# Chunk stage of an RWKV-7 time mix: inverse levels on the 32 changed columns, masks applied while leaving PSUM

## What is computed

```
def step(S, inp):
    r_t, w_t, k_t, v_t, a_t, b_t = inp
    sa = jnp.einsum('bhij,bhj->bhi', S, a_t)
    S = (S * w_t[:, :, None, :] + sa[..., None] * b_t[:, :, None, :]
         + v_t[..., None] * k_t[:, :, None, :])
    return S, jnp.einsum('bhij,bhj->bhi', S, r_t)

seq_in = tuple(u.transpose(1, 0, 2, 3) for u in (r_h, w_h, k_h, v_h, -kk, kk * a_h))
S0 = jnp.zeros((B, N_HEADS, HEAD_DIM, HEAD_DIM), jnp.float32)
_, y = lax.scan(step, S0, seq_in)
```

## Time and profile before

| | us |
|---|---|
| median of three runs | 1816.76 (1816.45 to 1817.86) |
| the profiled execution | 1815.43 |
| its span in the trace | 1813.7 |
| TensorE busy | 1668.9 (92%) |
| VectorE busy | 868.4 (48%) |
| ScalarE busy | 609.5 (34%) |
| GpSimd busy | 227.0 (13%) |

### The profile page before, as it was taken

The page is one execution under the profiler, slowest core; times in us unless marked ns, Lnnn a source line. Parts: engine busy times, 40 slices in busy tenths (PEclk is TensorE's granted clock), DMA queues, the critical chain, the costliest instruction groups (busy, mean ns, idle before and its releaser), DMA issues. The chain is left out here.

```text
span 1813.7 us, 35585 instructions
## 1 busy us (share of the span) xinstructions
PE 1668.9 (92%) x15964; PEld 1513.4 (83%) x15964; DVE 868.4 (48%) x1089; ACT 609.5 (34%) x826; POOL 227.0 (13%) x238
## 2 busy tenths in 40 slices
PE   4999998999999999989999688788877999999997
PEld 3999897899999999879989687778735888888886
DVE  3454453344433443467565466545575544334432
ACT  2454353332221223255664222212143333222222
POOL 2010010001000104000002232322111011001100
PEclk9999997899999999979899899989988999999998
DMA  3211110233332323242221100000012333323331
GB/s 96 67 57 53 59 53 18 71 94 91 90 99 82 91 86 108 61 143 70 68 72 47 49 3 3 3 3 3 3 45 69 94 93 102 96 81 95 102 104 48
DMA packets 214169, 121.38 MB, mean 67 GB/s; under 512 B 8744, under 2 KB 209600, under 8 KB 213760
## 3 DMA queue, kind: packets, MB, share of 16 engines
q1 hardware_dynamic: 213712, 118.98, 22.3%
q10 hardware_dynamic: 304, 0.08, 0.0%
HBM read 112.29 MB, written 6.76 MB: 66 GB/s over the span
## 5 line engine op out<-in xcount | busy, mean ns | idle before, releaser
L124 ACT ACTIVATE w_hi<-w_raw 128x1024 fp32r<-128x1024 f32 (+1 forms) x194 | 215.5, 1111 | 603.8 <-PE psg L731 483.0
L731 PE MATMUL psg<-x_hi,w_hi 128*128 128x264 f32 (+1 forms) x1096 | 357.7, 326 | 9.3 <-PEq L2398 9.3
L731 PE MATMUL psg<-x_lo,w_hi 128*128 128x264 f32 (+1 forms) x1096 | 357.9, 327 | 0.0
L731 PE MATMUL psg<-x_hi,w_lo 128*128 128x264 f32 (+1 forms) x1096 | 356.9, 326 | 0.0
L128 DVE TENSOR_TENSOR w_lo<-w_raw,w_hi 128x1024 fp32r<-128x1024 f32 (+1 forms) x194 | 250.4, 1291 | 139.0 <-ACT w_hi L124 138.8
L731 PEld LDWEIGHTS psg<-x_hi,w_hi 128*128 128x128 f32 x1096 | 206.5, 188 | 29.0 <-issue 10.3
L731 PEld LDWEIGHTS psg<-x_lo,w_hi 128*128 128x128 f32 x1096 | 206.5, 188 | 18.3 <-issue 0.2
L731 PEld LDWEIGHTS psg<-x_hi,w_lo 128*128 128x128 f32 x1096 | 207.1, 189 | 17.6
L731 PE MATMUL psg<-mid_hi,w_hi 128*128 128x264 f32 (+1 forms) x451 | 146.3, 324 | 0.0
L731 PE MATMUL psg<-mid_lo,w_hi 128*128 128x264 f32 (+1 forms) x451 | 146.0, 324 | 0.0
L731 PE MATMUL psg<-mid_hi,w_lo 128*128 128x264 f32 (+1 forms) x451 | 145.7, 323 | 0.0
(11 more groups left out here) (362 smaller groups left out, 3431.0 us busy)
## 6 DMA issues: line engine op xcount, KB each, us to landing
w_raw<-in_w_ffn_in_dram SPq DMA_DIRECT2D x88, 512.0 KB, 3.8
w_raw<-in_w_ffn_out_dram SPq DMA_DIRECT2D x32, 704.0 KB, 4.5
w_raw<-in_w_qkv_dram SPq DMA_DIRECT2D x24, 512.0 KB, 3.7
w_raw<-in_w_rkv_dram SPq DMA_DIRECT2D x24, 512.0 KB, 3.9
w_raw<-in_w_o_attn_dram SPq DMA_DIRECT2D x8, 512.0 KB, 4.1
w_raw<-in_w_o_rwkv_dram SPq DMA_DIRECT2D x8, 512.0 KB, 3.9
v_first<-v_pair SPq DMA_DIRECT2D x8, 264.0 KB, 2.1
res_kept<-res SPq DMA_DIRECT2D x1, 2112.0 KB, 7.8
```

Of the source, the lines that this page charges most:

```text
L124: k.nc.scalar.activation(k.w_hi[j][:, 0:kt, :], k.raw[j][:, 0:kt, :], ACT.Copy).then_inc(k.hi_ready[j].h, 1)
L731: done = k.nc.tensor.matmul(k.psg[:, 2 * j + c, 0:size], w[:, t, :], x, start=t == first and n == 0, stop=t == last and n == 2)
```

## The change

In the chunk stage:

- The products of a level are made only for the 32 columns (of 64) that the level changes: xt changes in the right block of each pair of blocks, xs in the left one. `block_cols` picks them as the moving operand, so that 64 stationary columns meet 32 moving ones. At level 3 the xs product has 16 moving columns and 64 stationary ones, where it was 32x32.
- The mask is no longer put on L before the product, by GpSimd, but on T after it: VectorE's `next_t` multiplies T with the mask `cross` on its way out of PSUM into `turned`, whose other half stays zero. The tiles `turned` and half of `vc` are cleared once, by GpSimd. ScalarE's copies of T are gone except at level 4 (`quarter`). `low` itself is the stationary operand.
- `l_products` makes three products a head instead of two: the odd columns of L transposed, the even columns of L (32 each, for the first xt and xs) and all of L. The identity's columns in xt and xs are written by ScalarE (`eyes`), at the end of the step before.
- `turn_v` becomes eight full transposes. ScalarE takes over the copies of V and of y.
- Other PSUM banks. The opening products wait for y and the first state update of the step before, no longer for the last xt and av.
- Another order: `chain_w` after level 0's first half, `chain_u` after level 1's first half, `chain_y_state` after level 1, `chain_s` ahead of level 4. On VectorE `products` comes behind the state's updates, and `quads` is split into `keys` and `reads`.
- `across` returns its rows unchanged: the products of a head stay in the rows of that head.

The diff, cut to its core:

```diff
@@ def chunk_stage(k, r):
+        def across(rows):
+
+            return rows
...
@@ ScalarE, step
-                        copy_t(n, 0)
+                        act.wait_ge(tv_d.h, n + 1)
+                        nc.scalar.activation(uv[p][C:P, :, :].rearrange("p (two m) c -> p m two c", two=2),
+                                             pair_ps[C:P].rearrange("p b (m two c) -> p (b m) two c", two=2, c=C), ACT.Copy)\
+                            .then_inc(uvv_r.h, 1)
...
@@ GpSimd, step
-                    if prep:
-                        pool.wait_ge(low_r.h, n + 1)
-                        for e in range(levels_of(n)):
-                            nc.gpsimd.tensor_tensor(es[e][:], low[:], over_rows(ch.level[e + 1]),
-                                                    ALU.mult).then_inc(e_r.h, 1)
...
@@ VectorE
+                def next_t(n, e):
+                    w = 2 ** (e + 1)
+                    dve.wait_ge(t_d.h, level_count(n, e))
+                    mask = ch.cross[e][:].rearrange("p (o g w) -> p o g w", o=1, w=w)
+                    nc.vector.tensor_tensor(block_cols_of_pairs(turned[e], w, 1), t_ps.rearrange("p m (g w) -> p m g w", w=w),
+                                            mask.broadcast_to([P, KT, HC // w, w]), ALU.mult).then_inc(t_r.h, 1)
...
+                        keys(n, 1)
+                        if levels_of(n) == levels:
+                            next_t(n, 3)
+                        reads(n, p, 1)
+                        if levels_of(n) == levels:
+                            next_xt(n, p, 3)
+                            next_xs(n, 3)
...
@@ TensorE, l_products
-                    for h, m, rows in heads:
-                        mm(lt_ps[rows, m, :], bk[rows, m, 0, :], ar[p][rows, m, 0, :], start=True, stop=True)
...
+                    for m in range(KT):
+                        for h, _, rows in heads[2 * m:2 * m + 2]:
+                            mm(first_t_ps[rows, m, :], bk[rows, m, 0, :], block_cols(ar[p][rows, m, 0, :], 1, 1)
+                               .rearrange("p g w -> p (g w)"), start=True, stop=True)
+                        for h, _, rows in heads[2 * m:2 * m + 2]:
+                            mm(first_s_ps[across(rows), m, :], ar[p][rows, m, 0, :], block_cols(bk[rows, m, 0, :], 1, 0)
+                               .rearrange("p g w -> p (g w)"), start=True, stop=True)
...
@@ TensorE, turn_v
-                        last = mm(pair_ps[C:P, m // 4, (m % 4) * P:(m % 4) * P + P], vc[:, m, :], k.ident[:],
-                                  start=True, stop=True)
+                        last = nc.tensor.transpose(pair_ps[:, m // 4, (m % 4) * P:(m % 4) * P + P],
+                                                   vc[:, m, :, :].rearrange("p a c -> p (a c)"), k.ident[:])
...
@@ TensorE, times_x
-                            last = mm(t_ps[rows, m, :], es[e][rows, m, :], xt[p][rows, m, :], start=True, stop=True)
+                            last = mm(t_ps[to, m, :].rearrange("p (g w) -> p g w", w=w), low[rows, m, :],
+                                      block_cols(xt[p][rows, m, :], w, 1), start=True, stop=True)
```

More of the change, by code:

```diff
@@ L1891, in chunk_masks @@
                  (ch.eye[rows, :], ALU.not_equal, 1.0, 0, [[1, C]], -1),
[L1892 to L1898, removed]
+                 (ch.first_t[rows, :], ALU.is_equal, 0.0, 0, [[-2, C // 2]], 1),
+                 (ch.first_s[rows, :], ALU.is_equal, 0.0, -1, [[-2, C // 2]], 1)]
+        for e, mask in enumerate(ch.cross):
+            w = 2 ** (e + 1)
+            view = mask[rows, :].rearrange("p (g w) -> p g w", w=w)
+            steps.append((view, ALU.is_ge, 0.0, 0, [[-2 * w, C // (2 * w)], [0, w]], 1))
+            steps.append((view, ALU.is_ge, 0.0, w - 1, [[2 * w, C // (2 * w)], [0, w]], -1))
         for view, op, fill, base, pattern, by in steps:
@@ L1954, in level_count, with t_count @@
             return e + 1 if type(n) is int and n == 0 else levels * n + (first_levels - levels + e + 1)
+        def t_count(n, e):
+            return e + 1 if type(n) is int and n == 0 else (levels - 1) * n + (first_levels - levels + e + 2)
         def xt_count(n, j):
@@ L2102, in next_x @@
                     elif e < levels_of(n) - 1:
[L2103 to L2113 removed]
+                        part = block_cols_of_pairs(xs[:], w, 0)
@@ new lines, in next_xs, with masks, pairs @@
+                        nc.vector.tensor_tensor(part, part, dx_ps.rearrange("p m (g w) -> p m g w", w=w),
+                                                ALU.subtract).then_inc(xs_r.h, 1)
+                quad_ps = pair_ps.rearrange("p b (m c) -> p b m c", c=2 * C)
+                def masks(mask):
+                    rows, _ = mask.shape
+                    return mask.rearrange("p (o a c) -> p o a c", o=1, a=1).broadcast_to([rows, 2, KT // 2, C])
+                def pairs(half):
+                    return slice(half * KT // 2, (half + 1) * KT // 2)
@@ L2159, in step @@
                                                 ALU.mult).then_inc(state_r.h, 1)
+                    if ahead:
+                        products(n + 1, q)
+                    if prep and levels_of(n) == levels:
+                        next_xt(n, p, levels - 1)
                 products(0, 0)
+                dve.wait_ge(zero_r.h, len(turned) + 1)
                 steps(dve, step)
@@ L2247, in x_times @@
+                    if e == levels - 1:
+                        pe.wait_ge(quarter_r.h, n)
+                    else:
+                        pe.wait_ge(t_r.h, t_count(n, e))
                     pe.wait_ge(xs_r.h, xs_count(n, e))
                     settle()
-                    for h, m, rows in heads:
-                        if e == levels - 1:
-                            low_rows = slice(rows.start, rows.start + C // 2)
-                            last = mm(lt_ps[low_rows, m, C // 2:C], xs[low_rows, m, 0:C // 2], tt[low_rows, m, C // 2:C],
-                                      start=True, stop=True)
-                        else:
-                            last = mm(lt_ps[rows, m, :], xs[rows, m, :], tt[rows, m, :], start=True, stop=True)
@@ L2337, in step @@
                             x_times(n, 3)
-                            times_x(n, p, 4)
-                            a_v(n, p)
-                            x_times(n, 4)
+                        else:
+                            quads(n, p, 1)
                     if chain and prep:
                         chain_s(c, q)
+                    if prep:
+                        if levels_of(n) == levels:
+                            times_x(n, p, levels - 1)
+                        a_v(n, p)
+                        if levels_of(n) == levels:
+                            x_times(n, levels - 1)
                 steps(pe, step)
```

238 lines of the change are left out of this document (127 added, 111 removed).

## The result

| | before | changed kernel |
|---|---|---|
| median | 1816.93 us (12 runs, 1815.44 to 1818.66) | 1826.49 us (12 runs, 1815.71 to 1836.48) |
| ratio | | 1.0054, 95% interval 1.0033 to 1.0076 |
| profiled execution | 1815.43 (span 1813.7) | 1836.48 (span 1834.8) |

The change makes the kernel slower by half a per cent. Its runs also spread over 21 us, where those of before spread over 3 (up to 11 in the sets taken beside the later runs). The profiled one is the longest of them, 10 us over the median, so its trace shows more of the loss than a typical run has.

The account below looks back on a forecast made before the run. TensorE's work and waits were taken to bound the chunk stage. Eight full steps at -1.0 us and a first at -1.3 gave about -9.5, so about 1807 us from 1816.8; range 1785 to 1878.

Parts of the forecast that it names:

- rival 1: Chunk stage: TensorE's clock falls around narrow products and waits; net +45 - 10, about 1850 us (1820 to 1900); chance 0.36.
- TensorE's list sets the pace: Chunk stage: a step is TensorE's work plus its waits; GpSimd or ScalarE savings count only where TensorE waits.
- The group prices: TensorE in a step: 0.95 us per 32-column group and added opening group, V transposes -0.9, last xs product +0.3.
- Rival 3: Fourteen groups per step: the moving side paces, 0.62 us each, -35 to -45 in all, about 1772 us; chance 0.09.
- The waits: TensorE's waits per full step: 2.6 us after, against 3.74 and a short one of about 0.1; taken as -1.2.
- The 1.3 at level 3: New wait before level 3's second half: masked T queued on VectorE behind `keys(n, 1)`, 1.3 to 1.4 us.
- the 0.5 at the opening products: New wait: `products(n + 1)` behind the state updates, 2.9 us against 2.3 us of TensorE's work.
- The two of 0.2: Waits left before the first halves of level 0 (0.82 before) and level 3 (0.33 before).
- the 0.44 of "issue": Wait in the products that open the next step, forecast to stay at 0.44 us.
- The sum: -1.0 us per full step, -8 for eight, -1.3 for the first; about -9.5 us; forecast's chance 0.46.
- the halved moving operand is worth nothing on TensorE: Fourteen groups per step: the stationary load paces them, so 0.95 us each stays; -1 us a step at best.
- Rival 2: No gain arrives: new waits as long as those removed, or a dearer loop jump; 1813 to 1819 us; chance 0.09.

Follow-up runs that it names:

- wide: The changed kernel with all 64 moving columns again in the opening products and levels 0 to 3: 1784.82 us, ratio 0.9824.
- wide_early: The changed kernel with 64 moving columns in the opening products and levels 0 and 1 only, levels 2 and 3 narrow: 1802.39 us, ratio 0.9926.
- swap_wide_tfirst_apart: `swap_wide_tfirst` with all of a level's second-half products for xt issued before all for xs, not in turns: 1767.13 us, ratio 0.9724.
- swap: The changed kernel with `across` returning the partner head's rows, so a pair's products use four quarters of the array: 1768.91 us, ratio 0.9733.
- swap_wide_tfirst: `swap` with 64 moving columns again and T of level 3 masked ahead of the key mask: 1748.85 us, ratio 0.9624.

## Why the prediction was wrong

The forecast was 1807 us, faster; it came out at 1826.5, slower, within the range of 1785 to 1878. What happened is rival 1.

- **TensorE's list sets the pace:** right. 64 us less for GpSimd and 56 less for VectorE brought nothing by themselves.
- **The group prices:** right. 0.92 for a group with 32 moving columns (0.88 to 0.95 forecast), 1.02 for `turn_v` (0.98), 2.95 for the three opening groups (1076.35 to 1079.30; 0.98 each, 0.95 forecast). The second half of level 3 takes 1.97 us (1099.21 to 1101.18) where 0.95 and 0.62 were before: +0.4, forecast +0.3. Rival 3 (0.62 a group) is out.
- **The waits:** right in kind. The 1.3 at level 3 measured 1.33 to 1.42, the 0.5 at the opening products 0.5. The two of 0.2 and the 0.44 of "issue" do not stand by themselves in the undisturbed step of `wide`. Idle time there is 1.96 us (28.9 less 26.94) against 3.87 before: -1.9, forecast -1.2. The reason given for part of it, masks on GpSimd beside VectorE, holds only for additions with both operands in SBUF.
- **The sum:** the sign was right and the size too small. `wide` is the change as the sum priced it, narrow columns being worth nothing, and it gives -32 us, not -9.5. By the starts of the first instruction of a step on VectorE: a first step of 23.2 instead of 27.8 us (-4.6; I had -1.3), the two steps over a jump 33.8 and 34.7 instead of 39.0 and 38.5 (-9.0 together), the five other steps -12.0 together (28.9 to 29.9 us each, where an undisturbed one took 31.0; I had -1.0 each), 42.7 instead of 48.6 us from the last start to the next stage's first product (-5.9), and a first start 1.1 us later: -30.4, and the spans differ by 30.6. The waits of before had a second price that I had not put into the sum, the falls of the clock around them: at the jump had 0.92. By the clock of each step, the stage loses about 23 us before and 8 in `wide`. That makes some 15 of the 32 us the clock and some 17 shorter waits, where I had 9.5 (an estimate: it takes all the time at the lower level as TensorE's work). TensorE's busy time in an undisturbed step is 26.9 to 27.5 us in `wide` and 27.1 to 27.3 before: no change, where I had summed +0.35. Where that third of a microsecond went stays open.
- **The step that failed** is "the halved moving operand is worth nothing on TensorE", with 0.95 as its upper bound. It has a price, +42 us as the change orders it (1826.5 less 1784.8), and none of it is in the groups at full clock, which gain a little by it (0.92 for 0.95 us). The loss stood only in rival 1, and it was given 0.36 because "the waits get shorter in sum, and dense products still stand between the narrow ones". The sum of the waits was the wrong thing to look at: with one wait of 1.3 to 1.4 directly ahead of the narrowest products of the step the clock falls in most steps, as it does in the earlier trace rows around 1238, 1.4 to 2 us behind the end of a wait of 0.97 (at 1236.04). And the dense products between did not bring it back: in the rows above it stays low from 1170 until shortly before 1204.
- **Rival 1's own sum:** 64 us for the low clock less 20 already lost less 10. Measured +42 and -32, so its price was nearly right, and its 1850 is too high mainly for the gain set against it. That the price fits is luck in part, because its place, from level 3 to the start of the next step, is only half of it: the first step, which has no such wait in it, runs at 0.50 almost throughout (33.6 us instead of 23.2). Its support in the attention stage was weak, too: of the 64 products in the 15.5 us of the earlier trace rows, 24 move 16 or 32 columns, but by their starts they fill only 4.2 us, and the others move 144 to 512. The runs here, not that row, show what narrow products do.
- **The clock and busy time:** the Trainium skill ("TensorE: Matmul & The Clock Gate", "What's actually happening") lets the clock follow how busy TensorE has been. Here 30.00 of 30.00 us busy pass at 0.50, and `wide` holds 0.97 with 162 of 180 us busy: by busy time the trace does not agree.
- **Rival 2** (no gain arrives) is out: it arrives and is overruled.
- **Not priced at all:** that the heads of a pair stay in the same rows while the two products of a level are now issued in turns. I took every group at 0.95 wherever it lies; in turns and in different quadrants two cost 1.06.

Still open is why the changed kernel's runs spread over 21 us; `wide` spreads over 1 and `wide_early` over 20, so it goes with the falls of the clock, but no run shows what decides between them. Open, too, is why narrow products get or keep the lower clock; the runs show only that they do.

## What to carry to other kernels

Where the stationary load sets the price of a small product, halving its moving operand saves next to nothing (0.92 for 0.95 us a group) and can cost the clock; look at the granted clock of such stretches before narrowing, and keep waits away from just ahead of the narrowest products. A wait is priced by its length and by the work that runs at the lower clock behind it. Two kinds of 64x64 products should lie in different quadrants and be issued in turns.

## What the hardware showed that was not expected

- With 32 moving columns, TensorE was busy for 30.00 of 30 us and stayed at 0.50. From the stage's first product on it stayed there for some 40 us; with 64 columns the same products left that level within 4.
- 64x64 products in four quadrants run beside each other: 1.06 us for 64 instructions against 1.97 in two. Both the place and the order are needed (1.84 with the order undone).
- In the versions whose products use four quadrants, pauses put down to "issue" appear inside and ahead of groups. Without those at the jumps they come to 0.4 us in `wide` from 1010 to 1275, 4.3 in `swap_wide_tfirst_apart`, 6.0 in `swap` and 9.5 in `swap_wide_tfirst`, up to 1.2 us each. What causes them was not tested. In `swap_wide_tfirst_apart`:

```profile
1063.87 0.45 PE L2328 MATMUL psg<-xs,w_raw 64*64 64x64 f32 x8
1065.02 0.80 PE L2328 MATMUL psg<-xs,w_raw 64*64 64x64 f32 x19 [0.71 <-issue]
```

- GpSimd beside VectorE costs VectorE 0.64 us for an addition of 128x256 with both operands in SBUF, and nothing where one operand is in PSUM (0.42 us in both kernels).
